# Light expert tiles with one unsplit down matrix and row halves summed ahead of the transposes, and the expert stage written out without loops

## The reference

```
for e in range(N_EXPERTS):                       # 32
    a = silu(hf @ w_e_gate[e]) * (hf @ w_e_up[e])    # 1024 -> 512
    out = out + gates[:, e:e + 1] * (a @ w_e_down[e])  # 512 -> 1024
```

## Time and profile before

| | |
|---|---|
| median of 3 runs | 1677.28 us (1676.32 to 1678.29) |
| profiled execution, own time | 1676.23 us |
| its span | 1674.6 us, mean granted TensorE clock 0.994 |
| busy: PE, weight load, VectorE, ScalarE, POOL | 1626.1, 1426.8, 1325.7, 1035.5, 81.1 us |
| transfers | 393.24 MB, mean 235 GB/s |
| chain of waits by engine | PE 65%, VectorE 14%, DMA 10%, ScalarE 5%, issue 5% |
| expert stage | about 320 to 890 us |
| costliest groups | splits on VectorE L2411, 358 times, 810.5 us; on ScalarE L1686, 675.3 us |

### The profile page before, as it was taken

The page is one execution under the profiler, slowest core; times in us unless marked ns, Lnnn a source line. Parts: engine busy times, 40 slices in busy tenths (PEclk is TensorE's granted clock), DMA queues, the critical chain, the costliest instruction groups (busy, mean ns, idle before and its releaser), DMA issues.

```text
span 1674.6 us, 27905 instructions
## 1 busy us (share of the span) xinstructions
PE 1626.1 (97%) x10552; PEld 1426.8 (85%) x10552; DVE 1325.7 (79%) x1514; ACT 1035.5 (62%) x1153; POOL 81.1 (5%) x94
## 2 busy tenths in 40 slices
PE   7999999999999999999998989999999999999998
PEld 7999999888887677777767978999999999998887
DVE  6577878855799999999986897687767879687776
ACT  5355765645789999999986464454344394453443
POOL 0000000000000000000006210000000020000000
PEclk9999999999999999999998999999999999999999
DMA  9643344366899999999998434446554565445650
GB/s 323 209 140 102 102 151 130 134 252 214 302 415 418 422 422 423 422 422 423 422 412 282 145 126 137 140 152 221 180 188 153 162 201 177 128 163 177 199 175 25
DMA packets 186667, 393.24 MB, mean 235 GB/s; under 512 B 6992, under 2 KB 151120, under 8 KB 162000
## 3 DMA queue, kind: packets, MB, share of 16 engines
q1 hardware_dynamic: 181600, 374.32, 61.1%
q0 software_dynamic: 4976, 17.67, 2.8%
HBM read 381.34 MB, written 10.62 MB: 234 GB/s over the span
## 4 chain that ended last, share of the span: by engine, by line
PE 65%; DVE 14%; DMA 10%; ACT 5%; issue 5%; POOL 0%; SPq 0%; DVEq 0%; ACTq 0%; POOLq 0%
PE ps L956 9%; DMA raw<-w_e_up_dram 8%; DVE wlo L2411 7%; PE ps L1142 6%; PE ps L962 5%; PE ps L669 4%; PE ps L674 4%; PE ps L670 4%; PE ps L971 4%; PE ps L1091 3%; PE ps L1097 3%; PE ps L1093 2%; ACT whi L1686 2%; PE ps L687 1%; PE ps L688 1%
## 5 line engine op out<-in xcount | busy, mean ns | idle before, releaser
L2411 DVE TENSOR_TENSOR wlo<-raw,whi 128x2048 fp32r<-128x2048 f32 (+2 forms) x358 | 810.5, 2278 | 138.3 <-ACT whi L1686 131.2
L1686 ACT ACTIVATE whi<-raw 128x2048 fp32r<-128x2048 f32 (+2 forms) x358 | 675.3, 1890 | 298.1 <-PE ps L962 113.7
L1091 PE MATMUL ps<-whi,xh 128*128 128x512 f32 x528 | 160.3, 396 | 0.0
L956 PE MATMUL ps<-xb,whi 128*128 128x512 f32 x672 | 160.2, 391 | 0.0
L669 PE MATMUL ps<-xh,whi 128*128 128x256 f32 x608 | 151.7, 289 | 4.6 <-DVE arena L2493 2.6
L670 PE MATMUL ps<-xl,whi 128*128 128x256 f32 x608 | 149.0, 285 | 0.0
L956 PEld LDWEIGHTS ps<-xb,whi 128*128 128x128 f32 x672 | 124.1, 188 | 24.3
L1097 PE MATMUL ps<-wlo,xh 128*128 128x512 f32 x528 | 143.3, 396 | 1.4 <-DVE wlo L2411 1.4
L669 PEld LDWEIGHTS ps<-xh,whi 128*128 128x128 f32 x608 | 117.7, 194 | 6.0 <-DVE arena L2493 3.0
L1097 PEld LDWEIGHTS ps<-wlo,xh 128*128 128x128 f32 x528 | 97.2, 188 | 29.5 <-DVE wlo L2411 9.6
L670 PEld LDWEIGHTS ps<-xl,whi 128*128 128x128 f32 x608 | 117.9, 194 | 0.3
(11 more groups left out here) (509 smaller groups left out, 3184.5 us busy)
## 6 DMA issues: line engine op xcount, KB each, us to landing
raw<-w_e_gate_dram SPq DMA_DIRECT2D x64, 1024.0 KB, 10.1
raw<-w_e_up_dram SPq DMA_DIRECT2D x64, 1024.0 KB, 10.3
raw<-w_e_down_dram SPq DMA_DIRECT2D x64, 1024.0 KB, 10.3
raw<-ffn_w_gate_up_dram SPq DMA_DIRECT2D x44, 1024.0 KB, 5.1
raw<-w_in_dram SPq DMA_DIRECT2D x30, 1024.0 KB, 5.9
raw<-ffn_w_down_dram SPq DMA_DIRECT2D x22, 1024.0 KB, 4.9
raw<-xa_w_kv_dram SPq DMA_DIRECT2D x16, 1024.0 KB, 5.5
raw<-xa_w_q_dram SPq DMA_DIRECT2D x8, 1024.0 KB, 5.1
```

Of the source, the lines that this page charges most:

```text
L956: nc.tensor.matmul(ps[:, bank + b, :], wh[:, k, b * P:b * P + P], xb[:, k, :, :].rearrange("p a t -> p (a t)"), start=k == 0, stop=False, ...
L1091: nc.tensor.matmul(o, h[:, k, :], wh[:, k, :], start=part == 0 and k == 0, stop=False)
L1686: nc.scalar.activation(whi[u % HL][:, 0:n], raw[u % RAW][:, 0:n], ACT.Copy).then_inc(hi_ready, 1)
L2411: v.tensor_tensor(wlo[u % HL][:, 0:n], raw[u % RAW][:, 0:n], whi[u % HL][:, 0:n].bitcast(F32), ALU.subtract).then_inc(lo_ready, 1)
```

## The change

In a light tile:

- The first down half is used as loaded. Its units (`whole`) get no `whi` and no `wlo`; PE multiplies `raw` by an unsplit `hid_whole`, four float32 matmuls of 512 columns in place of 12 (`down_whole`). Its `raw` buffer is free when PE is done with it, and SP waits for that (`unit_used`). All counts of `hi_ready` and `lo_ready` skip such units (`parts_to`).
- `gate_out` and `up_out` copy only PSUM rows 64 to 127, to partitions 0 to 63. VectorE adds rows 0 to 63 to them (`halves_added`), ScalarE takes the silu of 64 x 512 (`silu_summed`), VectorE multiplies (`hidden_summed`), and PE turns the product by four transposes. ScalarE then writes two pieces, `hid_whole` and the high part of the other half; VectorE the low part of that half only.
- The order in `tile` is new: both copies ahead of the split of u+6, both sums ahead of it on VectorE.

In the stage: all loops are written out. An order of ranks (`ORDER`) is introduced, which here is the old one. Tiles 1 and 2 store to fixed rows aside (`ASIDE`) in a longer `compact`; for that VectorE shifts the row numbers with 11 more operations between `xl_ready` and the gates, PE does one more small matmul for `aside_at`, and POOL copies two pieces of 1 MB from `xT` to `compact` after its second load of `x`. Start rows are read right at each window.

```diff
+                def down_whole(u, m):
+                    s = FIRST[m]
+                    pe.wait_ge(raw_landed[u % RAW], 16 * (u // RAW + (u % RAW > 0)))
+                    pe.wait_ge(r_hid_whole, sum(light(a) for a in range(m + 1)))
+                    pe.wait_ge(r_y, s)
+                    weights = wview_raw(u, 2, D)
+                    for n in range(2):
+                        for k in range(2):
+                            mm = nc.tensor.matmul(ps[0:SLOTS, 4 + n, :], hid_whole[s % 2][:, k, :],
+                                                  weights[:, k, 512 * n:512 * n + 512], start=k == 0, stop=False)
+                    mm.then_inc(unit_used, 1)
...
                 if i is not None:
+                    sp.wait_ge(lo_ready, i * step + parts_to(u - RAW))
+                elif u - RAW in whole:
+                    sp.wait_ge(unit_used, u - RAW + 1)
                 elif u >= RAW:
+                    sp.wait_ge(lo_ready, parts_to(u - RAW))
...
-                with pe.Fori(0, (TILES - HEAVY - 3) // LOOP) as i:
-                    for m in range(HEAVY + 1, HEAVY + 1 + LOOP):
-                        tile(m, i)
+                for m in range(1, TILES):
                     tile(m)
...
+                        hi(u + 2)
+                        hi(u + 3)
+                        hi(u + 4)
+                        if twice(m - 2):
+                            y_there(u, m - 2)
+                        hidden_high(m - 1)
+                        if not twice(m - 2):
+                            y_there(u, m - 2)
+                        hi(u + 5)
+                        gate_out(u + 3, s)
+                        up_out(u + 4, s)
+                        hi(u + 6)
+                        silu_summed(m)
...
+                def halves_added(m):
+                    s, n = FIRST[m], sum(light(a) for a in range(m))
+                    gate, up = sil[s % 2][0:SLOTS, :], hid[s % 2][0:SLOTS, :]
+                    dve.wait_ge(pair_out, 2 * n + 1)
+                    v.tensor_tensor(gate, ps[0:SLOTS, s % 2, :], gate, ALU.add).then_inc(gate_summed, 1)
+                    dve.wait_ge(pair_out, 2 * n + 2)
+                    link(v.tensor_tensor(up, ps[0:SLOTS, 2 + s % 2, :], up, ALU.add))
...
+                    lo(u + 2)
+                    lo(u + 3)
+                    lo(u + 4)
+                    hidden_low(m - 1)
+                    if light(m):
+                        for a in ahead[:1]:
+                            dve.wait_ge(unit_used, u - 2)
+                            window(a, m + 1)
+                        lo(u + 5)
+                        halves_added(m)
+                        lo(u + 6)
+                        hidden_summed(m)
...
-            v.tensor_tensor(both, ident[:, 0:SLOTS], ident[:, SLOTS:], ALU.add).then_inc(both_set, 1)
+            v.tensor_copy(aside_at, ps[:, 7, 65:68])
...
-            v.tensor_copy(rows_i, rows_f)
+            v.tensor_scalar(aside_by[:, 0:1], aside_at[:, 0:1], -1.0, -2.0 * T, ALU.mult, ALU.add)
+            link(v.tensor_tensor(aside_by[:, 1:2], aside_at[:, 0:1], aside_at[:, 1:2], ALU.subtract))
+            v.tensor_scalar(aside_by[:, 1:2], aside_by[:, 1:2], float(T), None, ALU.add)
+            v.tensor_scalar(aside_by[:, 2:3], aside_at[:, 1:2], float(T), None, ALU.add)
+            link(v.tensor_scalar(moved, rows_f, 2.0 * T, None, ALU.add))
+            for a in range(3):
+                link(v.tensor_scalar(shift, rows_f, aside_at[:, a:a + 1], aside_by[:, a:a + 1], ALU.is_ge, ALU.mult))
+                link(v.tensor_tensor(moved, moved, shift, ALU.add))
+            v.tensor_copy(rows_i, moved)
...
+            for a in range(2):
+                pool.dma_start(compact[(2 + a) * T:(3 + a) * T, :],
+                               t["xT"].rearrange("(a b) n -> a (b n)", b=DC // 2)).then_inc(y_stored, 16)
```

More of the change, by code:

```diff
@@ L50, with starts_of, twice, light @@
 FEW = (PAIRS_OUT - 1) // (SLOTS // 2)
+ORDER = tuple(range(TILES))
+ASIDE = {1: 0, 2: 1}
+def starts_of(rank):
+    return (2 * rank, 2 * rank + 1) if rank < TWICE else (rank + TWICE,)
+def twice(m):
+    return ORDER[m] < TWICE
+def light(m):
+    return ORDER[m] >= HEAVY
+FIRST = [sum(len(starts_of(r)) for r in ORDER[:m]) for m in range(TILES + 1)]
 def passes(m):
-    return (2 * m, 2 * m + 1) if m < TWICE else (m + TWICE,)
+    return tuple(range(FIRST[m], FIRST[m + 1]))
+START_AT = [a for r in ORDER for a in starts_of(r)]
+def rows_of(m):
+    return P if not light(m) else SLOTS if ORDER[m] < FEW else SLOTS // 2
 D_FF = 2816
@@ L205, in build @@
         start_i, order_i = table_i[:, 0:PASSES], table_i[:, PASSES:]
-        both = area(58 * T + 960, SLOTS)
+        aside_at = area(58 * T + 960, 3)
+        aside_by = area(58 * T + 963, 3)
+        moved, shift = area(58 * T + 966, 2, 2), area(58 * T + 970, 2, 2)
         zeros = area(60 * T + 320, P)
@@ L401, in build, with parts_to, last_in, wview_raw @@
         trio0 = [0, ffn[0][1]]
+        whole = {moe + 6 * (m + 1) + 2 if m < TILES - 1 else moe + 6 * TILES - 2 for m in range(TILES) if light(m)}
+        def parts_to(u):
+            return u + 1 - sum(w <= u for w in whole)
+        def last_in(u):
+            return next((w for w in range(u - HL, -1, -HL) if w not in whole), None)
+        def wview_raw(u, kc, n):
+            return raw[u % RAW][:, 0:kc * n].rearrange("p (k n) -> p k n", k=kc)
         def wview(buf, u, kc, n):
@@ L586, in load_experts @@
                 load(p0 + 3, wu[1][e])
[L588 to L601, removed]
-                    for m in range(HEAVY + 1, HEAVY + 1 + LOOP):
-                        tile(m, i)
-                for m in range(HEAVY + 1 + (TILES - HEAVY - 1) // LOOP * LOOP, TILES):
-                    tile(m)
-                e = expert(TILES - 1)
+                for m in range(1, TILES):
+                    u, before, e = p0 + 6 * m - 2, e, expert(m)
+                    load(u, wg[0][e])
+                    load(u + 1, wu[0][e])
+                    load(u + 2, wg[1][e])
+                    load(u + 3, wu[1][e])
+                    load(u + 4, wdn[0][before])
+                    load(u + 5, wdn[1][before])
                 for a in range(2):
@@ L1098, in unit @@
                                                   stop=part == 1 and k == 3)
-                        if m < TWICE and up and part and s % 2 == 0:
+                        if twice(m) and up and part and s == FIRST[m]:
                             mm.then_inc(first_done, 1)
@@ L1892, in tile_twice @@
                     ahead = passes(m + 1)
-                    row = [row_start(s) for s in ahead]
                     hi(u + 2)
@@ L1902, in tile_twice, with tile @@
                     hi(u + 5)
[L1903 to L1904 removed]
+                    act.wait_ge(first_done, sum(twice(a) for a in range(m + 1)))
+                    window(ahead[0], m + 1)
                     hi(u + 6)
[L1906 to L1907 removed]
+                    for s in ahead[1:]:
+                        window(s, m + 1)
                     hi(u + 7)
[L1910 to L1911 removed]
+                def tile(m):
+                    if twice(m):
```

390 lines of the change are left out of this document (176 added, 214 removed).

## The result

The changed kernel took 1679.16 us (median of 20 runs, 1675.42 to 1682.52), the kernel before 1676.76 in the same rounds (20 runs, 1672.3 to 1678.29): a ratio of 1.0016, with the 95% interval 1.0008 to 1.0023. That is some 2.7 us slower (1.3 to 3.9), and inside the 0.2% that the prediction called no change. The same kernel once more, in another set of rounds, gave 1.0007 (0.9998 to 1.0016), which by itself would not show a slowdown. The profiled execution, 1676.46 us with a span of 1674.8, is one of the short ones among the 20, and hardly differs from the profiled execution of before; what follows compares stretches and not spans.

A forecast was written before the change was run, and what follows sets the result against it. Light tiles were taken as bound by their bytes at 422 GB/s, heavy tiles by PE. Terms 0 + 0.8 + 1.9 - 0.3 - 0.3 = +2.1 us on the median 1677.28 gave 1679.3 us, range 1673.5 to 1686.0.

The forecast's parts named there:

- Light tiles: 25 light tiles of the expert stage: engine work falls, the bytes stay the same, so 0 us.
- rival of shorter tiles: Light tiles follow PE down from 15.20 to some 14.4 us, 24 tiles give 19 us: 1660; chance 0.12.
- longer loop: New waits between engines make a light tile exceed its transfers; 0.3 us over costs 7 us: 1686.5; chance 0.10.
- The ring: Light tiles' weight loads: refill issued 2.9 us later, 4.8 us of cover left, DMA does not run dry: 0 us.
- Unrolling: Written-out light tiles: 0.35 MB of instructions push the loads by 0.8 us, bounds 0 and 2.
- Eleven operations: Added VectorE operations ahead of the expert stage delay PE's first unit by 1.9 us, between 1.4 and 2.8.
- rival "hidden": Added operations ahead of the stage cost nothing, PE held by something else at 329.8: 1677.4; chance 0.05.
- The 2.1 us named beside the 1.9: Added time ahead of the stage if nearly all added VectorE operations before 326.32 wait for POOL's cast.
- Handover: Tile 8, slices 11 and 12: y's copy comes a split earlier, 0.3 us won of 1.1 at most.
- The two copies of 1 MB in DRAM: Issued by POOL near 245 us, with room in transfers idle after 275 us: 0, at most 1 us.
- Tail: Last tile: first down matrix 0.7 slower, turning 1.3 faster, one split gone: -0.3 us, between -1.5 and +1.
- Clock rival: PE's added pause before its first expert unit drops its clock, costing 1.7 us: 1681.0; chance 0.20.

The follow-up runs named there:

- a_small_stores: Changed kernel with every light tile's store cut to 32 rows, rows 32 to 63 of tiles 7 to 14 left out; 1677.80 us, ratio 1.0001.
- a_hold_4: Changed kernel with the raw buffer of the unsplit down matrix given back three units later; 1797.54 us, ratio 1.0735.
- b_no_loops: Kernel before with all loops of the expert stage written out, tiles unchanged; 1677.62 us, ratio 1.0013.
- a_mem_later: Changed kernel with the load of memT held until PE is done with the second down half of tile 29; 1678.87 us, ratio 1.0016.
- a_all_later: Changed kernel with row and gate arithmetic behind VectorE's first hidden-row splits of tile 0 and memT's load held later; 1676.77 us, ratio 1.0007.
- b_eleven_ops: Kernel before with only the 11 small VectorE operations added ahead of the integer row numbers, results unused; 1677.54 us, ratio 1.0011.
- a_rows_later: Changed kernel with row arithmetic and integer copy moved behind VectorE's first hidden-row splits of tile 0; 1677.94 us, ratio 1.0016.

## Why the prediction was right

The forecast was 1679.3 us, the median 1679.16. Its sign, the mechanism of the stage and the place of most of the loss hold. That it came within 0.2 us is luck: four of its terms are off by 0.3 to 1.3 us, one is missing, its terms add up to 1679.4 and not 1679.3, and its base, 1677.28, was 1676.76 in the rounds of the result.

- **Light tiles, 0 us: right.** Periods of 15.20 and 15.50 at 422 GB/s, with VectorE and ScalarE a tenth less busy, and a_small_stores moves the period by the bytes of a store alone. This refutes the rival of shorter tiles, and, with no period over the old one by more than 0.05 us but those four in which instructions came, that of a longer loop. Unsplit matmuls were forecast at 0.86 us and took 0.895; the transposes 0.5, and took 0.62.
- **The ring, 0 us: right, its margin wrong.** The issue came 1.9 us later (8.0 to 6.07 us ahead of the landing before it), not 2.9. But the 4.8 us of cover said to be left were not there: an issue one unit later, 2.1 us nearer to the landing before it, cost 0.8 in a late tile. The step that failed is that of 10.24 us from issue to landing everything but one transfer of 2.53 was counted as waiting; a_hold_4 shows some 1.7 us that are neither, and the rate fell with more left than that. What is left is under 2.1 us (6.07 less 3.96), and 1.3 if all behind its end costs in full. Had PE released the buffer one unit later than it did, the forecast would have missed by almost 20 us.
- **Unrolling, +0.8: right in kind, mis-sized.** 18 packets and 0.21 MB came instead of some 20 and 0.35 MB, and the price was 1.4 us, 1.5 in b_no_loops; its bounds, 0 and 2, held it. Bytes over bandwidth is not the price of a packet.
- **Eleven operations, +1.9: 1.6 in the changed kernel and 1.58 alone.** The three with two scalars stepped at 0.32 us, the other linked ones at 0.20, dearer than the 0.19 of the row used; the unlinked ones at 0.06 to 0.07; and the first of the row fell into the time in which VectorE stood beside POOL's cast (3.0 us from 324.59 to the last at 327.61, 1.06 of them there). That nothing was slack behind them (rival "hidden", 0.05) was right in this direction only. The sign named for it, a first unit at 331.7 to 332, was missed: it came at 331.15, 0.3 of that because the routing ended earlier. The 2.1 us named beside the 1.9 were further off: one added operation met the cast, and its wait took the place of the old one.
- **Handover, -0.3: not shown.** The slices 11 and 12 went from 415 and 418 to 408 and 417 GB/s, so nothing was won there.
- **The two copies of 1 MB in DRAM, 0: nothing seen.** The routing's selection matrix starts 0.3 us earlier than before, but its start lies between 319.2 and 321.8 us in the profiles of this document, so a cost of less than a us would not show.
- **Tail, -0.3: wrong in sign.** +1.0 us from tile 30's landing to the last y, from the load of `memT`, whose issue hangs on an operation of VectorE that the change made earlier. I followed SP's queue past the moved steps and not POOL's. Without the overlap the stretch is 0.1 (a_mem_later) and 1.4 us (a_all_later) shorter than before, so the steps that the term named may well have given what it said.
- **Not in the sum: what the gathers give back.** 1.6 + 1.4 + 1.0 is 4.0 us; the last y of this pair is 4.0 later, counted from the selection matrix (3.7 on the clock), and the sum behind the gathers 1.5 (1.2). So the measured terms less what comes back make 1.5, the forecast 2.1, the medians 2.4 apart: errors of both signs, and noise of the same size, are how the last two came so near.
- **Clock rival (0.20): not seen at its place.** Behind the new pause of 1.45 us before 331.15 the granted clock stayed at 1.00, and so it did behind 1.69 us in b_eleven_ops and 2.50 in a_mem_later. Its point of decision, between pauses of 1.60 and 2.29 us, is refuted too: at 883 us a pause of 1.43 to 1.49 us is followed by the lower level in four profiles and by the full one in seven.

What stays open: how much of the changed kernel's loss at the end belongs to each step. One profile each shows the stretches, but the medians of a_rows_later and a_mem_later, each with one cost removed, did not fall with them.

## What to carry to other kernels

Where a stage lasts as long as its bytes take, work taken off the engines buys nothing, but it still moves the issue of every load that hangs on the order of that work: look for the later loads that come forward, as well as for the ring's that go back. Measure a ring's margin by delaying its refill on purpose by one unit, not by subtracting transfers from the time between issue and landing. And before moving work off a path, look at what its successor waits for next: here a second wait stood 0.2 us behind.

## What was not expected of the hardware

- Written-out loops cost 1.4 to 1.5 us for 18 to 22 more packets of instructions in a stage that saturates the transfers, 0.07 to 0.08 us a packet, where their bytes would take 0.03 (that it is the packets is argued, not shown).
- An issue 4 us ahead of the landing of the last queued load was too late to keep 422 GB/s; one 6 us ahead was in time. A load from SP moved its first byte 0.95 us after the issue and landed 0.7 us after its last.
- With the same pause of 1.4 to 1.5 us, TensorE's clock fell to the 1.2 GHz level in some executions and stayed at 2.4 GHz in others; eight records then took 5.31 us instead of 3.62. Behind a pause of 2.50 us at another place it stayed at 2.4 GHz.
